# Three of the next expert's six weight units pass through dead space and are copied into the weight ring by GpSimd

## The reference, cut to what matters

```python
gsel, idx = lax.top_k(aff.transpose(0, 2, 1), C)
xs = jax.vmap(lambda hb, ib: hb[ib])(h, idx)
hid = jax.nn.silu(jnp.einsum('becd,edf->becf', xs, w_gate)) * jnp.einsum('becd,edf->becf', xs, w_up)
ye = jnp.einsum('becf,efd->becd', hid, w_down) * gsel[..., None].astype(h.dtype)
```

## Time and profile before

| | |
|---|---|
| median of 3 runs | 1974.2 us (1972.06 to 1977.78) |
| the profiled execution, its own time | 1975.05 us |
| its span, first to last instruction | 1973.1 us |
| TensorE busy | 1721.6 us (87%) |
| VectorE, ScalarE, GpSimd busy | 628.7, 327.0, 128.9 us |
| weight transfers on SP's queue | 482.37 MB |
| mean rate of all transfers | 271 GB/s |

### The profile page before, as it was taken

One profiled execution on the slowest core, in us unless ns is written; L12 is line 12 of the kernel. 1 busy time (PEld: TensorE's weight loads), 2 busy tenths in 40 slices (PEclk: granted clock), 3 DMA queues, 4 the chain that ended last, 5 costly groups with the idle time before them and its releaser, 6 DMA issues.

```text
span 1973.1 us, 60455 instructions
## 1 busy us (share of the span) xinstructions
PE 1721.6 (87%) x28403; PEld 1363.8 (69%) x28403; DVE 628.7 (32%) x1051; ACT 327.0 (17%) x674; POOL 128.9 (7%) x157
## 2 busy tenths in 40 slices
PE   4999988986998989898939999889499989898993
PEld 2555456546998888888825544655499989888983
DVE  1299367142111101010125983833511101010112
ACT  2100045320110101010030002543101101010001
POOL 3000000000000000000010000001000000000001
PEclk9999989997999999999969999999699999999997
DMA  9246540445999999999941452214399999999995
GB/s 344 95 143 241 213 160 1 149 160 186 375 399 389 398 389 399 388 399 388 395 169 43 171 208 74 91 58 171 115 384 387 400 387 399 386 398 387 399 388 215
DMA packets 154440, 534.70 MB, mean 271 GB/s; under 512 B 5938, under 2 KB 6355, under 8 KB 154387
## 3 DMA queue, kind: packets, MB, share of 16 engines
q1 hardware_dynamic: 138880, 482.37, 63.5%
q0 software_dynamic: 12320, 42.47, 7.4%
q10 hardware_dynamic: 3186, 9.12, 1.2%
HBM read 509.30 MB, written 24.64 MB: 271 GB/s over the span
## 4 chain that ended last, share of the span: by engine, by line
PE 55%; DMA 30%; DVE 8%; SPq 3%; issue 2%; ACT 1%; POOL 0%; DVEq 0%; POOLq 0%; ACTq 0%
DMA weight_ring<-in_w_gate_dram 26%; PE ps L737 16%; PE ps L504 14%; PE ps L643 7%; PE ps L754 6%; PE ps L541 3%; SPq L354 2%; PE ps L447 2%; DVE neg_m L1199 2%; DMA weight_ring<-in_w_mod_dram 1%; DMA weight_ring<-in_w_down_dram 1%; PE ps L603 1%; PE ps L767 1%; DVE weight_ring L1235 1%; PE ps L663 1%
## 5 line engine op out<-in xcount | busy, mean ns | idle before, releaser
L737 PE MATMUL ps<-v_sb,weight_ring 128*64 128x80 f32 x16384 | 613.4, 238 | 75.9 <-DMA weight_ring<-in_w_gate_dram 55.2
L737 PEld LDWEIGHTS ps<-v_sb,weight_ring 128*64 128x64 f32 x16384 | 598.6, 141 | 93.8 <-DMA weight_ring<-in_w_gate_dram 58.6
L754 PE MATMUL ps<-mix,weight_ring 128*64 128x80 f32 x8192 | 294.0, 233 | 7.7 <-DMA weight_ring<-in_w_down_dram 4.0
L754 PEld LDWEIGHTS ps<-mix,weight_ring 128*64 128x64 f32 x8192 | 286.3, 137 | 14.7 <-issue 10.2
L504 PE MATMUL ps<-mix,weight_ring 128*128 128x128 f32 (+1 forms) x1024 | 282.8, 437 | 4.7 <-DVE mix L1094 4.7
L504 PEld LDWEIGHTS ps<-mix,weight_ring 128*128 128x128 f32 x1024 | 156.2, 191 | 140.5 <-issue 135.3
L1361 DVE TENSOR_TENSOR mix<-mix,ps 128x320 f32<-128x320 f32 x64 | 28.3, 484 | 645.0 <-PE ps L737 645.0
L1123 DVE SCALAR_TENSOR_TENSOR weight_ring<-u_gate,conv_cols,weight_ring 128x655 f32<-128x655 f32 x240 | 195.3, 897 | 0.0
L643 PE MATMUL ps<-weight_ring,mix 128*128 128x512 f32 x320 | 141.7, 597 | 0.0
L1368 DVE SCALAR_TENSOR_TENSOR qk<-ps,gsel,gate 80x1024 f32<-80x1024 f32 x32 | 40.9, 1280 | 284.6 <-PE ps L767 284.6
L988 ACT ACTIVATE mix<-ps 128x320 f32<-128x320 f32 x64 | 24.5, 435 | 542.5 <-PE ps L737 542.5
(11 more groups left out here) (179 smaller groups left out, 1170.6 us busy)
## 6 DMA issues: line engine op xcount, KB each, us to landing
weight_ring<-in_w_gate_dram SPq DMA_DIRECT2D x64, 2048.0 KB, 24.6
weight_ring<-in_w_up_dram SPq DMA_DIRECT2D x64, 2048.0 KB
weight_ring<-in_w_down_dram SPq DMA_DIRECT2D x64, 2048.0 KB, 26.6
weight_ring<-in_w_mod_dram SPq DMA_DIRECT2D x24, 2048.0 KB, 8.2
weight_ring<-in_w_in_dram SPq DMA_DIRECT2D x10, 2048.0 KB, 13.7
weight_ring<-in_w_out_dram SPq DMA_DIRECT2D x4, 2048.0 KB, 9.7
x_res<-x_tile POOLq DMA_DIRECT2D x10, 512.0 KB, 3.4
x_unit<-x_norm ACTq DMA_DIRECT2D x10, 512.0 KB, 2.6
```

The lines of the kernel that those rows point to most:

```text
L737: last = nc.tensor.matmul(ps[c * HALF:(c + 1) * HALF, 2 * (i % 2) + f // BLK, f % BLK * CAP:(f % BLK + 1) * CAP], w[:, kk, o:o + HALF], pi ...
L754: last = nc.tensor.matmul(ps[c * HALF:(c + 1) * HALF, 4 + d // BLK, d % BLK * CAP:(d % BLK + 1) * CAP], w[:, kk, o:o + HALF], hid[:, k, :] ...
```

## The change

Three new places for a weight unit, called relays, in space that is dead while experts run: relay 0 in `qk`, relay 1 in `mix` behind its first 1024 columns, relay 2 over `u_gate` and the front of `v_sb` (now one tensor). For every expert but the first, units 0, 1 and 2 are loaded into the relays and then copied by GpSimd into their ring slots, when PE has used the slot's former unit. Units 3, 4 and 5 are loaded straight into the ring as before. What stood in the relays' space moves: `picked` and `added` to `x_tile`, `silu_g` to `conv_tmp`, `result_t` to `o_tok`, `h2_t` and `picked_t` to the end of `v_sb`, the final gain to the space of the rotary tables. The first gather now also waits until the residual rows in `x_tile` are stored. Which half of `w_gate` or `w_up` a unit holds changes by `UNIT_HALF`. Cut to its core:

```diff
+RELAYS = 3
+UNIT_HALF = (0, 1, 1, 0, 0, 1)
...
-        picked = qk_flat[0:CAP, 0:D]
-        added = qk_flat[0:CAP, 2 * D:3 * D]
+        relay = [qk_flat[:, 0:UNIT], mix_flat[:, D:D + UNIT], u_values[:, 0:UNIT]]
+        assert UNIT <= CH * U_LEN + TILES * BANK - D
         x_tile = sb("x_tile", [P, 2, D])
+        picked, added = x_tile[0:CAP, 0, :], x_tile[0:CAP, 1, :]
...
-        expert_loaded = [signal(f"expert_loaded{i}", EXPERTS, 16) for i in range(6)]
+        relay_loaded = [signal(f"relay_loaded{i}", EXPERTS - 1, 16) for i in range(RELAYS)]
+        relay_ready = [signal(f"relay_ready{i}", 16 + EXPERTS - 1) for i in range(RELAYS)]
+        expert_loaded = [signal(f"expert_loaded{i}", EXPERTS, 16) for i in range(RELAYS, 6)]
...
+            def first_unit(l, i):
+                sp.dma_start(ring[:, UNIT_SLOTS[l][i], :].rearrange("p (k n) -> p k n", k=KD // 2), expert_src(l, 0, i))\
+                  .then_inc(relay_ready[i].sem, 16)
+
+            def relay_unit(l, e, i):
+                sp.dma_start(relay[i].rearrange("p (k n) -> p k n", k=KD // 2), expert_src(l, e, i))\
+                  .then_inc(relay_loaded[i].sem, 16)
...
-                for i in range(6):
+                for i in range(3):
                     if i < 2:
                         sp.wait_ge(*mod_rows_done.at(l, units - 1 + i))
-                    elif i == 2:
+                    else:
                         sp.wait_ge(*pv_done.at(l, ATT))
                         sp.wait_ge(*gates_transposed.at(l, 2))
                         sp.wait_ge(*conv_out_ready.at(l, 1))
-                    elif i == 4:
-                        sp.wait_ge(*out_lo_used.at(l, 1))
-                    elif i == 5:
-                        sp.wait_ge(*out_done.at(l, TILES))
-                    expert_unit(l, 0, i)
-                with sp.Fori(1, EXPERTS) as e:
-                    for i in range(6):
-
+                    first_unit(l, i)
+                expert_unit(l, 0, 3)
+                relay_unit(l, 1, 0)
+                sp.wait_ge(*out_lo_used.at(l, 1))
+                expert_unit(l, 0, 4)
+                sp.wait_ge(*out_done.at(l, TILES))
+                expert_unit(l, 0, 5)
+                relay_unit(l, 1, 1)
+                sp.wait_ge(*x2_ready.at(l, TILES))
+                relay_unit(l, 1, 2)
+
+                def ring_units(e):
+                    for i in range(RELAYS, 6):
                         sp.wait_ge(*expert_used.at(l, e * 6 + (i - 5)))
                         expert_unit(l, e, i)
+
+                with sp.Fori(2, EXPERTS) as e:
+                    for i in range(RELAYS):
+                        sp.wait_ge(*relay_ready[i].at(l, e + 15))
+                        relay_unit(l, e, i)
+                    ring_units(e - 1)
+                ring_units(EXPERTS - 1)
...
                     for i in range(4):
-                        pe.wait_ge(*expert_loaded[i].at(l, e + 1))
+                        if i < RELAYS:
+                            pe.wait_ge(*relay_ready[i].at(l, e + 16))
+                        else:
+                            pe.wait_ge(*expert_loaded[i - RELAYS].at(l, e + 1))
...
                 pool.wait_ge(*unit_stored.at(l, TILES))
+                pool.wait_ge(*residual_written[0].at(l, 3))
+                pool.wait_ge(*residual_written[1].at(l, 2))
                 gather(0)
...
                 gather(1)
-                pool.wait_ge(*residual_written[1].at(l, 2))
+
+                def move_relays(e):
+                    for i in range(RELAYS):
+                        pool.wait_ge(*relay_loaded[i].at(l, e))
+                        pool.wait_ge(*expert_used.at(l, (e - 1) * 6 + i + 1))
+                        nc.gpsimd.tensor_copy(ring[:, UNIT_SLOTS[l][i], :], relay[i]).then_inc(relay_ready[i].sem, 1)
+
+                move_relays(1)
                 for e in range(EXPERTS):
...
                     if e + 2 <= EXPERTS:
                         gather(e + 2)
+                    if e + 2 < EXPERTS:
+                        move_relays(e + 2)
```

More of the change, by code:

```diff
@@ L96, in build @@
         mix = sb("mix", [P, KD, N_TOK])
-        u_gate = sb("u_gate", [P, CH * U_LEN])
-        u = u_gate[:, :].rearrange("p (c n) -> p c n", c=CH)
+        u_values = sb("u_values", [P, CH * U_LEN + TILES * BANK])
+        u_gate, v_sb = u_values[:, 0:CH * U_LEN], u_values[:, CH * U_LEN:]
+        u = u_gate.rearrange("p (c n) -> p c n", c=CH)
         gate1 = u_gate[:, 0:2 * D].rearrange("p (v n) -> p v n", v=2)
@@ L102, in build @@
         qk_flat = qk[:, :, :, :].rearrange("p a h n -> p (a h n)")
-        picked = qk_flat[0:CAP, 0:D]
-        added = qk_flat[0:CAP, 2 * D:3 * D]
[L105 to L108, removed]
+        v_tok = v_sb.rearrange("p (t n) -> p t n", t=TILES)
+        h2_t = v_sb[:, TILES * BANK - D:].rearrange("p (k n) -> p k n", k=KD)
+        picked_t = v_sb[:, TILES * BANK - D:TILES * BANK - D + KD * CAP].rearrange("p (k n) -> p k n", k=KD)
         x_all = qk_flat.rearrange("p (t n) -> p t n", t=TILES)
@@ L128, in build @@
         o_tok = sb("o_tok", [P, 2, H, VD])
+        silu_g = conv_tmp[:, :, :].rearrange("p b n -> p (b n)")[:, 0:KD * CAP].rearrange("p (b n) -> p b n", b=2)
+        result_t = o_tok[:, :, :, :].rearrange("p b h n -> p (b h n)")[:, 0:KD * CAP].rearrange("p (k n) -> p k n", k=KD)
         o_sq = conv_tmp[:, 1, 0:BANK].rearrange("p (h n) -> p h n", h=H)
-        cos_sb = sb("cos_sb", [P, N_LAT])
-        sin_sb = sb("sin_sb", [P, N_LAT])
+        rope_sb = sb("rope_sb", [P, 2 * N_LAT])
+        cos_sb, sin_sb = rope_sb[:, 0:N_LAT], rope_sb[:, N_LAT:2 * N_LAT]
+        gain_rows = rope_sb[:, 0:D]
         past_k_t = sb("past_k_t", [P, DEPTH, H, PAST])
@@ L349, in expert_src @@
             def expert_src(l, e, i):
-                w, half = (w_gate, w_up)[i % 2] if i < 4 else w_down, i // 2 if i < 4 else i - 4
+                w, half = (w_gate, w_up)[i % 2] if i < 4 else w_down, UNIT_HALF[i]
                 return w[l, e].rearrange("(k p) n -> p k n", p=P)[:, half * 4:half * 4 + 4, :]
+            def first_unit(l, i):
[4 more added lines that the diff above has]
+                  .then_inc(relay_loaded[i].sem, 16)
             def expert_unit(l, e, i):
                 sp.dma_start(ring[:, UNIT_SLOTS[l][i], :].rearrange("p (k n) -> p k n", k=KD // 2), expert_src(l, e, i))\
-                  .then_inc(expert_loaded[i].sem, 16)
+                  .then_inc(expert_loaded[i - RELAYS].sem, 16)
             sp.dma_start(cond_rows[0:KD, :], c_ctx.rearrange("(k p) -> k p", p=P)).then_inc(cond_loaded.sem, 16)
@@ L733, in gate_up @@
                             for kk in range(KD // 2):
-                                k = (i // 2) * (KD // 2) + kk
+                                k = UNIT_HALF[i] * (KD // 2) + kk
                                 for c in range(2):
@@ L740, in gate_up @@
                                         w[:, kk, o:o + HALF], picked_t[:, k, :],
-                                        start=(k == 0 and f % BLK == 0), stop=(k == KD - 1 and f % BLK == BLK - 1))
+                                        start=(i < 2 and kk == 0 and f % BLK == 0),
+                                        stop=(i >= 2 and kk == KD // 2 - 1 and f % BLK == BLK - 1))
                         last.then_inc(expert_used.sem, 1)
```

16 lines of the change are left out of this document (6 added, 10 removed).

## The result

Six runs of the changed kernel have a median of 1964.53 us (1959.46 to 1967.89), beside 1977.08 us for the kernel before: a ratio of 0.9949, 95% interval [0.9937, 0.9962]. In a second comparison it was 0.9960 [0.9946, 0.9974]. By the ratios the change gains 8 to 10 us (the medians lie 12.6 us apart in the first comparison and 9.2 in the second), where 23 were forecast: right in sign, inside the range of 1944 to 1967, and by the ratios less than half the size.

A forecast was written before the change was run, and what follows sets the result against it. Weight transfers were taken to bound both expert stages. Three units moved ahead gain 16.0 us a layer, less 4.3 for the later first issue, 11.7; twice that, 23.4 us, gave 1951 us, range 1944 to 1967.

The forecast's parts named there:

- The relays were filled before expert 0: Before each layer's expert 0: three units' loads, 16 us from about 433.5, fit in idle DMA time, at no cost.
- the first gather was not delayed: POOL's first gather: its new wait for the residual's stores costs nothing, as it is held until 455.86 anyway.
- the copy: GpSimd's copy of a unit from relay to ring slot: taken as 4.0 us, between bounds of 3.5 and 6.0.
- the first issue: Start of each expert stage: SP's first weight issue comes 4.3 us later, as relay 0 must first be copied out.
- handing over: Two semaphore steps around the first copy of a stage, taken as 0.3 us of the 4.3 us delay.
- GpSimd's queue: Three copies are 12 us of each 33.7 beside scatter and gather; no cost while a copy is below about 9 us.
- Rival (a): GpSimd's copies are slow: gain only 8 to 19 us; at 6.0 us a copy 17 us, 1957; chance 0.17.
- The end of the stage: Last expert transfer stays unit 5 of expert 15, next layer's projection right behind; all of it moves earlier together.
- the waits would still be 24 us: PE's waits for weights fall from 35.5 to about 24 us, so transfers stay the bound and the gain isn't cut.
- The signs that I had named: Among them: PE's first late unit at about 565 us instead of 600, layer 0's stage 510 us instead of 522.
- (b): No gain, 1969 to 1980 us: each copy delays the stage's first transfers, or relay loads collide with first gather; chance 0.09.
- (e): Whole stage: relays filled ahead do not help if PE is the bound; gain capped at some 70 us; no chance given.

## Why the prediction was wrong in size

**What held.** The transfers bound the stage, at 394 GB/s and 5.66 us a unit: (942.61 - 466.76)/84. The relays were filled before expert 0 (windows above), the first gather was not delayed (4.00 us to land in the chain, before 3.95), the copy took 3.60 us where I took 4.0, the first issue came 3.6 and 4.1 us later where I took 4.3 (of the 0.3 us in it for handing over, the extract of the chain above shows 0.12 from PE to POOL and 0.15 from POOL to SP). GpSimd's queue kept up. For the copy the Trainium skill, "GPSIMD Engine Reference" (section 3.1), had led to an estimate of 3.5 us by its 1.03 cycles an element and of 6.1 by its 1.8: the first agrees within 3% of the 3.60 us measured. Rival (a), which stood on the select's row, did not come.

**What failed** is one step, "The end of the stage": "Before and after, the last transfer for experts is unit 5 of expert 15 ... All of it moves earlier together." The transfers moved earlier. But the step took for granted that PE stays right behind them. The prediction named unit 3 as the one that PE would meet late first, and did not ask which place that unit has in the new order. Unit 3 of each expert kept its place, and PE had an expert's whole work left, 33.8 us, when the last unit that it waited for in layer 0 landed, instead of 4.65 us. That the waits would still be 24 us, from which I concluded that the gain is not cut, was the same mistake: they are 31.2 us in layer 0 now, where 35.5 stood in the earlier trace rows:

```profile
PE ps L766 <- DMA weight_ring<-in_w_up_dram: 30.2, 11, 3.6
PE ps L784 <- DMA weight_ring<-in_w_down_dram: 1.0, 3, 0.4
```

They are nearly all for `w_up` now, which is unit 3, and for nothing of the relays. The signs that I had named would have shown it: PE's first late unit came not at 565 us but at 596.22, which is 139.3 us after the stage's start against 136.8 before. It is unit 3 of expert 4, the same unit that was late first before.

None of the rivals had this mechanism. (b), "no gain", had it only as a slow copy or a collision; (e) came nearest, with PE as the bound, but for the whole stage. That the measured time lies inside the range is no merit of the mechanism: the range reaches down to a gain of 8 us for slow copies, and the copies were not slow.

**What came in that was not in the sum.** The spans of the two profiled executions lie further apart than the medians, 1973.1 - 1957.7 = 15.4 us, and have to be taken in pieces. 6.3 us lie ahead of the first expert matmul (463.18 against 456.91), where a second profile of the same changed kernel, with a span of 1965.3 us, has 462.98: that is a difference between executions and not the change's. The stages account for 3.4 us. A further 4.2 lie between the layers. From the start of the last transposes of layer 0 to the first projection matmul it took 1023.75 - 985.04 = 38.7 us and now takes 1010.94 - 976.44 = 34.5. The rest, 1.5 us, is spread. In the second profile the stages are 2.8 us shorter than before and this stretch 4.0. The chains of the two kernels name the piece, before:

```profile
996.71 2.19 POOL qk L1415 x4
998.90 11.47 DMA qk<-x_res
```

and after:

```profile
987.84 2.19 POOL qk L1444 x4
990.03 7.84 DMA qk<-x_res
```

The rows of the residual are read back beside the next layer's weights. That part of those weights has landed before, as the transfers end early, is the likely reason, and no edit tests it alone. In the experiments this stretch goes with when the transfers end: 34.2 to 34.9 us in the four profiles with three relays and PE alone at the end, 36.8 to 39.5 in those, the kernel before among them, where the transfers run into it. The kernel with one relay does not fit: PE alone ends its stage, and it has 37.6. So other effects play a part. 3.4 + 4.2 = 7.6 us, and 2.8 + 4.0 = 6.8 in the second profile, is what the profiles explain of the 8 to 10 measured.

## What to carry to other kernels

When loads are the bound, as here, a spare buffer helps only if the unit that the consumer waits for comes earlier by it: number the transfers, before and after, and look at which number that unit has. Prefetching ahead of the unit that is late keeps the bound and only lets the transfers end early; then the stage ends with the consumer's whole lead still to be worked off. Spend the lead before the end: load far ahead at the start, and go back to the consumer's order as many steps from the end as it takes the transfers to catch up (here 16.9 us at 4.5 us an expert, four experts).

## What the runs showed of the hardware

GpSimd copies 128x4096 float32 in 3.60 us and VectorE in 2.29. GpSimd busy 72% of the time with copies in SBUF left the transfers at 395 GB/s, where they had 394 at 38%.

A thing not expected: with each copy done twice, one VectorE instruction became slow. Its timeline in an expert of that kernel:

```profile
649.99 3.60 POOL L1524 COPY weight_ring<-u_values 128x4096 f32<-128x4096 f32 x1
650.46 0.82 DVE L1383 TENSOR_TENSOR u_values<-ps,scale_x 128x640 f32<-128x640 f32 x1
651.31 2.95 DVE L1385 TENSOR_TENSOR u_values<-u_values,shift_x 128x640 f32<-128x640 f32 x1
```

The first operation, one input in PSUM, runs at its 0.82 us beside the copy. The second has both inputs in SBUF: it starts, and ends 0.67 us after the copy does (654.26 against 653.59), as if it had stood still until then. Its median over the kernel is 1966 ns and its longest 4028, where it is 826 at most in the changed kernel, whose copies are over before it begins. By the Trainium skill, "SBUF — State Buffer" (section "SBUF: two separate sides"), a VectorE operation with two SBUF inputs and a GpSimd operation that reads SBUF exclude each other for a whole instruction, and the trace agrees with its 2.95 us. PE waits for this operation 3.9 us in two waits in the whole execution, with single copies and with double ones, so it cost nothing here: it runs during the 9 us of `down` matmuls. The same section of the Trainium skill states that engine ports and DMA ports cannot contend. The rate of 395 GB/s with POOL at 72% agrees.
